# Up product of the gathered tokens: four expert blocks of a quarter's depth per weight slot in place of two of half the depth

## The chip, the cores and the metric

One core of one Trainium2 chip runs the kernel in one launch. The time is the device time of one execution in microseconds (us); several executions are timed and the median counts.

## What is computed

One step of a decoder layer with 2048 channels for 576 tokens: 512 of a prompt and 64 of eight samples. There are a pooling mixer and a retention mixer, a cross-attention to 256 memory tokens, and a PEER channel mixer. The change lies in the mixer of experts, which is cut here to what matters:

```python
q = (xb @ peer_wq).reshape(PEER_BLOCK, PEER_HEADS, 2, PEER_HALF)
s = jnp.einsum('thcd,hckd->thck', q, subkeys)
sv, si = lax.top_k(s, PEER_TOPK)
...
u = jnp.take(peer_u, expert, axis=0)
act = jax.nn.gelu(jnp.einsum('thkd,td->thk', u, xb), approximate=False)
vv = jnp.take(peer_v, expert, axis=0)
return jnp.einsum('thk,thkd->td', g * act, vv)
```

There are 8 heads and 16384 experts of one neuron each. The kernel doesn't gather rows of `peer_u`: it computes gelu(x u) for all experts, and picks what each token needs afterwards.

## The kernel before

**Tokens.** The first 320 tokens (ND) are dense: they go through all experts both up and down. The last 256 (NG) are "gathered": their up product is computed for all experts and stored in DRAM (`gelg`), from where single values are fetched by index, and their down product adds gathered rows of `peer_v` on VectorE. This text is about the up product of those 256 tokens. It takes place in the stage of the heads, on the tile `HLG`, which holds them as two column groups c of 128 tokens.

**Precision.** Every fp32 operand is split in a high part (fp32r) and a low part, and a product is three matmuls: high x high, high x low, low x high (the loop over wp and xp).

**The ring of weight slots.** All weights pass through four slots `WS[:, k]` of 128 partitions x 1024 columns, high and low. SyncE loads 512 KB into one of four raw buffers (two in `RAW`, one in `CS`, one in `AR`, `RAW3`) as soon as the slot four before has been split; ScalarE copies it to the high part (`high`, L902 to L908) once TensorE has released the slot (semaphore `used`) and the load has landed; GpSimd subtracts and writes the low part (`low_part`, L402 to L405); TensorE waits for `split_done`. ScalarE and GpSimd work in the order of the slots, and each instruction stands behind the one before it.

**The stage of the heads** (PE loop over EH = 8). For each head: two projections of queries, each over two slots, for all tokens (`projection`, moving tiles of 320 and 256 columns); the scores of the keys (L813, 20 small matmuls) in between; and an eighth of the expert blocks, 16 blocks of 128 experts, for the gathered tokens in `tokens_first` (L779 to L796). On VectorE the selection of the head's top 16 runs beside it (L1581 to L1628), after ScalarE has copied the scores (`sc_evac`).

In `tokens_first(h, j, hf)` a pair j of expert blocks takes four slots: SyncE loads for each block two slots, of channel halves 0 and 1 (`load_u` with `both_first`, so slots 0 and 1 hold half 0 of both blocks). TensorE moves 2 x 128 columns, the same 128 channels of both blocks out of two slots, past the stationary 128x128 tile of a token group:

```python
for wp, xp in ((0, 0), (0, 1), (1, 0)):
    ins = mm(to, HLG[:, c, xp, kb, :], WS[:, 2 * hf:2 * hf + 2, wp, k * P:(k + 1) * P], ...)
```

Both slots are needed at once and are released together. To refill them in time the handshake is by half slots: TensorE signals `used_q` after the first four of eight channel blocks, ScalarE copies the first 512 columns of both slots (`hi_q`), GpSimd splits these (`split_q`, L428), and then the second halves follow by `used`, `hi_done` and `split_done`. At the end of a pair ScalarE applies GELU to a bank of 512 columns (L1223) and stores 256 KB in `gelg` (L1225). There are 64 pairs, 8 per head (UPP).

**After it.** The softmax of the selected scores (ScalarE L1251, VectorE L1634 to L1636), nine transposes (L825), and then the stages of the dense tokens, in which GpSimd fetches values out of `gelg` (L440).

An older stage is used below for comparison, the projection of the memory values (L554): there the moving operand is 512 columns of a slot, 12 matmuls for each slot, and every slot is released alone.

## Time and profile before

| | |
|---|---|
| median of three runs | 4879.75 us (4876.03 to 4882.84) |
| profiled execution, its own time | 4868.53 us |
| span of its trace | 4866.4 us |
| mean granted clock of TensorE | 0.967 of full speed |
| TensorE matmuls, busy | 4551.1 us (94%), 31875 instructions |
| VectorE busy | 2297.8 us (47%) |
| ScalarE busy | 1584.6 us (33%) |
| GpSimd busy | 3099.6 us (64%) |
| matmuls of L793 | 6144, 740.5 us busy, 1788.7 to 2736.8 us (first and last start) |

Busy times are unions of an engine's instructions. A matmul's duration in the trace is its latency; matmuls overlap, so what one costs in a row of them is read from the distance of starts. In the timeline a row merges instructions of one line; the number in brackets is idle time ahead of it, with what ended it.

### The profile page before, as it was taken

The page shows a single profiled execution, that of the slowest core. Times are in us where ns is not written, and L with a number is a line of the kernel's source. Part 1 is how long each engine was busy: PE and PEld are TensorE (multiplying, and loading weights), DVE is VectorE, ACT ScalarE, POOL GpSimd, SP SyncE. Part 2 cuts the span into 40 slices and gives each one's busy share as a digit, 9 for nine tenths or more (in the row PEclk, how much of TensorE's full clock was granted, in tenths as well). Part 3 has the DMA queues.
Part 4 walks back from the last instruction along what each step waited for, and adds up shares of the span by engine and source line. Part 5 has one row for each costly group of instructions (what it writes and reads, how often), then busy time and mean ns, then how long its engine had stood idle before and what let it go on. Part 6 is the DMA issues. An engine that isn't in the chain of part 4 may idle for free.

```text
span 4866.4 us, 82443 instructions
## 1 busy us (share of the span) xinstructions
PE 4551.1 (94%) x31875; PEld 4401.3 (90%) x31875; DVE 2297.8 (47%) x3074; ACT 1584.6 (33%) x2194; POOL 3099.6 (64%) x1782
## 2 busy tenths in 40 slices
PE   7999999998998989999999888799999999999997
PEld 7799988897887979999999888799999999999997
DVE  3721322423001154444444555466666666666656
ACT  4422111222222134444444454233333333333333
POOL 6833222243221447777777766799999899998864
PEclk9999999999998999999999988899999999999998
DMA  6553222332555245555555556999999899999954
GB/s 217 191 93 103 97 97 87 107 120 105 186 200 177 83 146 173 173 173 172 173 174 174 156 158 176 334 342 344 344 342 346 322 347 341 341 344 357 347 187 140
DMA packets 466611, 1032.95 MB, mean 212 GB/s; under 512 B 136944, under 2 KB 227184, under 8 KB 433648
## 3 DMA queue, kind: packets, MB, share of 16 engines
q1 hardware_dynamic: 216080, 590.67, 36.1%
q0 software_dynamic: 45056, 268.60, 14.3%
q10 hardware_dynamic: 205280, 170.84, 10.8%
q8 instruction: 152, 2.49, 0.2%
q14 instruction: 43, 0.35, 0.0%
HBM read 935.25 MB, written 94.73 MB: 212 GB/s over the span
## 4 chain that ended last, share of the span: by engine, by line
issue 38%; POOL 35%; PE 18%; DMA 4%; DVE 2%; ACT 1%; another core or an unknown queue 1%; POOLq 0%; ACTq 0%; SPq 0%; DVEq 0%
POOL WS L404 23%; PE PS L864 9%; POOL WS L428 8%; PE PS L521 5%; POOL ROWS L450 3%; PE PS L793 2%; DMA AR<-in_vE 2%; POOL AR L440 2%; PE PS L839 2%; ACT WS L896 1%; DMA RAW<-in_vE 1%; DMA gel<-AR 0%; DVE AR L1371 0%; POOL AR L450 0%
## 5 line engine op out<-in xcount | busy, mean ns | idle before, releaser
L521 PE MATMUL PS<-HL,WS 128*128 128x288 f32 (+2 forms) x16896 | 2426.7, 304 | 127.3 <-DVE HL L1408 33.9
L521 PEld LDWEIGHTS PS<-HL,WS 128*128 128x128 f32 x16896 | 2371.5, 192 | 163.0 <-issue 110.4
L404 POOL TENSOR_TENSOR WS<-RAW,WS 128x1024 fp32r<-128x1024 f32 x490 | 1200.6, 2463 | 1354.7 <-ACT WS L896 1350.7
L864 PE MATMUL PS<-WW,WS 128*128 128x320 f32 x6144 | 941.8, 315 | 79.6 <-POOL WS L404 62.9
L864 PEld LDWEIGHTS PS<-WW,WS 128*128 128x128 f32 x6144 | 922.2, 192 | 98.6 <-issue 79.2
L896 ACT ACTIVATE WS<-RAW 128x1024 fp32r<-128x1024 f32 (+1 forms) x714 | 628.1, 919 | 1011.3 <-PE PS L521 360.2
L793 PE MATMUL PS<-WS,HL 128*128 128x256 f32 x6144 | 740.5, 283 | 0.0
L793 PEld LDWEIGHTS PS<-WS,HL 128*128 128x128 f32 x6144 | 738.3, 192 | 0.0
L1677 DVE SCALAR_TENSOR_TENSOR PS<-ROWS,AR,PS 128x2048 f32<-128x2048 f32 x206 | 483.8, 2349 | 77.1 <-DMA ROWS<-in_vE,AR 76.8
L404 POOL TENSOR_TENSOR WS<-AR,WS 128x1024 fp32r<-128x1024 f32 x182 | 452.3, 2489 | 42.6 <-ACT WS L896 41.7
L404 POOL TENSOR_TENSOR WS<-CS,WS 128x1024 fp32r<-128x1024 f32 x144 | 347.4, 2413 | 187.0 <-ACT WS L896 185.2
L1692 DVE TENSOR_TENSOR AR<-AR,PS 128x320 f32<-128x320 f32 x512 | 248.6, 486 | 435.7 <-PE PS L864 423.8
L896 ACT ACTIVATE WS<-CS 128x1024 fp32r<-128x1024 f32 (+1 forms) x256 | 223.0, 871 | 495.4 <-PE PS L864 257.2
L896 ACT ACTIVATE AR<-PS 128x512 f32<-128x512 f32 (+11 forms) x255 | 172.7, 719 | 560.5 <-PE PS L521 295.4
L428 POOL TENSOR_TENSOR WS<-RAW,WS 128x512 fp32r<-128x512 f32 x224 | 304.6, 1389 | 16.8 <-ACT WS L896 15.6
L896 ACT ACTIVATE WS<-AR 128x1024 fp32r<-128x1024 f32 (+1 forms) x294 | 259.8, 888 | 129.1 <-PE PS L521 53.3
L440 POOL DMA_INDIRECT AR<-gelg,AR x256 | 249.4, 974 | 70.6 <-issue 65.2
L1581 DVE MAX8 AR<-AR 128x8 f32<-128x128 f32 (+1 forms) x120 | 30.1, 324 | 488.8 <-ACT AR L896 487.6
L450 POOL DMA_INDIRECT ROWS<-in_vE,AR x206 | 200.2, 972 | 32.0 <-issue 25.5
L1232 ACT ACTIVATE AR<-PS 128x320 f32<-128x320 f32 x128 | 56.7, 443 | 449.9 <-PE PS L521 379.8
L1665 DVE TENSOR_TENSOR AR<-AR 128x320 f32<-128x320 f32 x128 | 193.9, 1566 | 0.1
L1677 DVE SCALAR_TENSOR_TENSOR PS<-AR,PS 128x2048 f32<-128x2048 f32 x50 | 117.6, 2353 | 115.4 <-DMA AR<-in_vE,AR 115.4
(160 smaller groups left out, 2883.3 us busy)
## 6 DMA issues: line engine op xcount, KB each, us to landing
RAW<-in_uT SPq DMA_DIRECT2D x256, 512.0 KB
RAW<-in_w_lin SPq DMA_DIRECT2D x218, 512.0 KB
CS<-in_uT SPq DMA_DIRECT2D x128, 512.0 KB
AR<-in_uT SPq DMA_DIRECT2D x128, 512.0 KB
RAW<-in_vE SPq DMA_DIRECT2D x128, 512.0 KB
CS<-in_vE SPq DMA_DIRECT2D x64, 512.0 KB
AR<-in_vE SPq DMA_DIRECT2D x64, 512.0 KB
AR<-in_w_lin SPq DMA_DIRECT2D x46, 512.0 KB
```

The source lines that it names most:

```text
L404: pool.tensor_tensor(WS[:, k, 1, :], raw(k, many, late), WS[:, k, 0, :].bitcast(F32), ALU.subtract)\
L428: pool.tensor_tensor(WS[:, k, 1, half], raw(k, True, True)[:, half], WS[:, k, 0, half].bitcast(F32), ALU.subtract).then_inc(S["split_done" ...
L440: pool.indirect_dma_start(out=GA[:, c, k:k + 1], out_offset=None, in_=values, in_offset=at(EL[:, c, k:k + 1]))\
L450: pool.indirect_dma_start(out=ROWS[b], out_offset=None, in_=rows, in_offset=at(VI[:, c, r:r + 1]))\
L521: ins = mm(to, WS[:, slot + hf, wp, k * P:(k + 1) * P], x, start=first and (wp, xp) == (0, 0), stop=last and wp == 1, skip_group_check=True)
L793: ins = mm(to, HLG[:, c, xp, kb, :], WS[:, 2 * hf:2 * hf + 2, wp, k * P:(k + 1) * P], start=(kb, c, wp, xp) == (0, 0, 0, 0), stop=kb == KB ...
L839: ins = mm(bank(4 + q % 2, P, off=P * k), BB[:, q % 2, k, :], AA[:, q % 2, k, :], start=True, stop=True, skip_group_check=True)
L864: ins = mm(bank(2 + d % 2, ND), WS[:, 2 * (q % 2) + b, vp, 512 * e + P * d4:512 * e + P * (d4 + 1)], W[:, 2 * b + e, wp, :], start=(b, e, ...
L896: copy = lambda out, in_, **kw: act.activation(out, in_, ACT.Identity, **kw)
L1665: tt(gi, gi, PP[:, e // 2, :, e % 2, :], ALU.mult).then_inc(S["w_done"], 1)
L1677: stt(ACC, ROWS[b], GA[:, c, r:r + 1], ACC, ALU.mult, ALU.add).then_inc(S["row_done"], 1)
L1692: tt(X[:, d, 0:ND], X[:, d, 0:ND], bank(2 + d % 2, ND), ALU.add).then_inc(S["v_free"], 1)
```

## The change

A quad j of four expert blocks now takes eight slots, and a slot holds a quarter of a half: 256 channels (two blocks of 128) of all four expert blocks. TensorE moves 4 x 128 = 512 columns out of one slot, past the same stationary tiles; each token group writes a bank of its own. There are 12 matmuls per slot, and the slot is released and refilled alone, through the same `used`, `hi_done` and `split_done` as elsewhere. The half-slot semaphores go. One GELU covers 1024 columns, and one store 512 KB. There are 32 quads, 4 per head (UPQ). The scores come after two slots, as before; ScalarE copies them after the high part that follows the third slot.

```diff
@@ SyncE
+            def load_quarters(quad, n):
+                for k in range(8):
+                    sp.wait_ge(S["split_done"], free(n + k, 4))
+                    sp.dma_start(raw(k % 4, True, True).rearrange("p (e w) -> p e w", e=4),
+                                 uT.rearrange("(b x) p w -> x b p w", x=2)[k // 4, bass.ds(4 * quad, 4), :, 256 * (k % 4):256 * (k % 4 + 1)]
+                                 .rearrange("b p w -> p b w")).then_inc(S[f"raw{k % 4}"], 16)
...
             with sp.Fori(0, EH - 1) as h:
-                load_u(h * (4 * UPP), h * H_HQ + (H_WQ + 4), 4 * UPP, both_first)
+                for j in range(UPQ):
+                    load_quarters(h * UPQ + j, h * H_HQ + (H_WQ + 4 + 8 * j))
@@ GpSimd
-            with pool.Fori(0, EH) as h:
-                for j in range(2):
-                    low_parts(h * H_HQ + (H_WQ + 4 * j), late=True)
-                for j in range(1, UPP):
...
-                                pool.tensor_tensor(WS[:, k, 1, half], raw(k, True, True)[:, half], WS[:, k, 0, half].bitcast(F32),
-                                                   ALU.subtract).then_inc(S["split_done" if at else "split_q"], 1)
+            with pool.Fori(0, EH * H_HQ // 4) as i:
+                low_parts(i * 4 + H_WQ, late=True)
@@ TensorE
-            def tokens_first(h, j, hf):
...
+            def tokens_first(h, j, quarters):
+                n = h * H_HQ + (H_WQ + 4 + 8 * j)
+                if quarters[0] == 0:
+                    pe.wait_ge(S["lin_evac"], h * (2 + UPQ) + (B_WQ + 2 + j + 1))
+                for q in quarters:
+                    pe.wait_ge(S["split_done"], n + split(q))
+                    for k in range(2):
+                        for c in range(2):
+                            for wp, xp in ((0, 0), (0, 1), (1, 0)):
+                                experts = WS[:, q % 4, wp, :].rearrange("p (e k n) -> p k e n", e=4, k=2)[:, k]
+                                ins = mm(tiles(bank(2 * (j % 2) + c)), HLG[:, c, xp, 2 * q + k, :], experts,
+                                         start=(q, k, wp, xp) == (0, 0, 0, 0), stop=(q, k, wp) == (7, 1, 1),
+                                         skip_group_check=True)
+                    ins.then_inc(S["used"], 1)
...
-                tokens_first(h, 0, 0)
+                tokens_first(h, 0, range(2))
...
-                tokens_first(h, 0, 1)
-                for j in range(1, UPP):
-                    for hf in range(2):
-                        tokens_first(h, j, hf)
+                tokens_first(h, 0, range(2, 8))
+                for j in range(1, UPQ):
+                    tokens_first(h, j, range(8))
...
-                    ins = pe.transpose(bank((3, 5, 6)[k], P, off=P * t), src[:, t, :], IDENT)
+                    ins = pe.transpose(bank(4 + k, P, off=P * t), src[:, t, :], IDENT)
@@ ScalarE
-                for hf in range(2):
-                    if j < UPP - 1:
-                        act.wait_ge(S["used_q"], h * (2 * UPP - 2) + (2 * j + hf + 1))
...
+                for q in range(8):
+                    act.wait_ge(S["used"], n + used(q + 1))
+                    high(n + (q + 4), q % 4, late=True)
+                    if (j, q) == (0, 2):
                         act.wait_ge(S["sk_done"], h + 2)
...
-                act.activation(GOG[:, e, :], bank(2 * e), ACT.Gelu).then_inc(S["lin_evac"], 1)
+                act.activation(GOG[:, e].rearrange("p s n -> p (s n)"), PS[:, 1024 * e:1024 * (e + 1)], ACT.Gelu)\
+                    .then_inc(S["lin_evac"], 1)
```

TensorE's order in the loop of the heads, from the last matmuls of the second query projection. L521 (L518 in the changed kernel) is the projection, L793 (L787) the up product, L813 (L805) the scores. Before:

```order
L521 MATMUL PS<-HL,WS 128x256
L783 REGISTER_ALU
L788 REGISTER_ALU
L793 MATMUL PS<-WS,HL 128x256 x48
L805 REGISTER_ALU
L806 REGISTER_ALU
L813 ISA
L813 MATMUL PS<-AR 128x128 x5
```

and in the changed kernel:

```order
L518 MATMUL PS<-HL,WS 128x256
L780 REGISTER_ALU
L782 REGISTER_ALU
L787 MATMUL PS<-WS,HL 128x512 x12
L782 REGISTER_ALU
L787 MATMUL PS<-WS,HL 128x512 x12
L797 REGISTER_ALU
L798 REGISTER_ALU
L805 ISA
L805 MATMUL PS<-AR 128x128 x5
```

48 matmuls of 256 columns over two slots have become twice 12 of 512 columns, with a wait ahead of each slot; the scores stand at the same slot. The rest of the head follows in the same manner, 12 matmuls per slot.

GpSimd's order in the same loop, with the waits: WS<-RAW, WS<-CS and WS<-AR are the subtractions for slots 0 and 1, 2, and 3. Before, from the second pair of a head on:

```order
L428 TENSOR_TENSOR WS<-RAW,WS 128x512 [waits hi_q]
L424 REGISTER_ALU
L428 TENSOR_TENSOR WS<-RAW,WS 128x512 [waits hi_q]
L426 REGISTER_ALU
L428 TENSOR_TENSOR WS<-RAW,WS 128x512 [waits hi_done]
L426 REGISTER_ALU
L428 TENSOR_TENSOR WS<-RAW,WS 128x512 [waits hi_done]
```

and in the changed kernel, the loop's whole body:

```order
L425 ISA
L413 TENSOR_TENSOR WS<-RAW,WS 128x1024 [waits hi_done]
L412 REGISTER_ALU
L413 TENSOR_TENSOR WS<-RAW,WS 128x1024 [waits hi_done]
L412 REGISTER_ALU
L413 TENSOR_TENSOR WS<-CS,WS 128x1024 [waits hi_done]
L412 REGISTER_ALU
L413 TENSOR_TENSOR WS<-AR,WS 128x1024 [waits hi_done]
L425 REGISTER_ALU
L425 COMPARE_AND_BRANCH
```

Four halves over two slots have become a whole slot each, and the loop turns every four slots, where it turned once per head.

## Rows read from the trace of the kernel before

**Rows 1.** stretches: us, busy us (count) of each engine, clock, DMA share, GB/s

```profile
1910.00:2030.00 120.00, 118.44 (x969) 118.26 (x968) 54.58 (x144) 49.88 (x81) 94.77 (x64) 1.00 0.55 176
150.00:226.00 76.00, 76.00 (x337) 62.93 (x336) 63.15 (x34) 38.73 (x47) 72.39 (x28) 1.00 0.64 210
```

**Rows 2.** groups, 1788 to 2740 us: shapes, count | busy us, mean ns | idle before

```profile
L793 PE MATMUL PS<-WS,HL 128*128 128x256 f32 x6144 | 740.5, 283 | 0.0
...
L428 POOL TENSOR_TENSOR WS<-RAW,WS 128x512 fp32r<-128x512 f32 x224 | 304.6, 1389 | 16.8 <-ACT WS L896 15.6
```

**Rows 3.** waits, 1788 to 2740 us: us in total, times, longest us

```profile
DVE AR L1581 <- ACT AR L896: 487.6, 8, 68.7
```

**Rows 4.** TensorE's timeline of one head: start us, us, operation, count [idle before]

```profile
2006.95 25.84 PE L521 MATMUL PS<-HL,WS 128*128 128x320 f32 x192 [1.56 <-issue]
2032.63 5.92 PE L793 MATMUL PS<-WS,HL 128*128 128x256 f32 x48
2038.38 2.39 PE L813 MATMUL PS<-AR 128*128 x20
2040.53 86.64 PE L793 MATMUL PS<-WS,HL 128*128 128x256 f32 x720
```

**Rows 5.** timeline of TensorE's weight loads in the value projection

```profile
149.87 76.12 PEld L554 LDWEIGHTS PS<-WS,HL 128*128 128x128 f32 x336
```

**Rows 6.** timeline of ScalarE and GpSimd, early in a head's expert slots

```profile
2033.53 1.07 ACT L896 ACTIVATE WS<-CS 128x1024 fp32r<-128x1024 f32 x1
...
2034.68 2.42 POOL L404 TENSOR_TENSOR WS<-CS,WS 128x1024 fp32r<-128x1024 f32 x1 [8.05 <-ACT WS L896]
...
2047.74 1.28 ACT L1223 ACT_TABLE_LOAD   x1
```

**Rows 7.** timeline of ScalarE and GpSimd in the value projection

```profile
163.43 1.01 ACT L896 ACTIVATE AR<-PS 128x1024 f32<-128x1024 f32 x1
163.82 5.26 POOL L404 TENSOR_TENSOR WS<-AR,WS 128x1024 fp32r<-128x1024 f32 x2
...
169.05 5.26 POOL L404 TENSOR_TENSOR WS<-RAW,WS 128x1024 fp32r<-128x1024 f32 x2
```

**Rows 8.** GpSimd's timeline during VectorE's one-hot work, first and last row

```profile
2076.08 3.79 POOL L428 TENSOR_TENSOR WS<-RAW,WS 128x512 fp32r<-128x512 f32 x2 [0.25 <-ACT WS L896]
...
2096.73 1.29 POOL L428 TENSOR_TENSOR WS<-AR,WS 128x512 fp32r<-128x512 f32 x1
```

**Rows 9.** timeline at the end of the stage

```profile
2737.19 1.06 ACT L896 ACTIVATE WS<-CS 128x1024 fp32r<-128x1024 f32 x1 [3.75 <-PE PS L793]
...
2739.10 0.58 ACT L1223 ACTIVATE AR<-PS 128x512 f32<-128x512 f32 x1
...
2742.45 0.82 DVE L1634 TENSOR_REDUCE AR<-AR 128x40 f32<-128x640 f32 x1 [32.60 <-ACT AR L1251]
...
2744.62 2.18 PE L825 MATMUL PS<-CST,AR 128*128 128x128 f32 x9 [7.55 <-DVE AR L1636]
...
2747.01 1.10 POOL L440 DMA_INDIRECT AR<-gelg,AR  x1 [4.03 <-DVE AR L1648]
```

**Rows 10.** DMA, 1788 to 2740 us: packets, MB, share; KB, us to landing

```profile
q1 hardware_dynamic: 40858, 148.82, 48.2%
q10 hardware_dynamic: 17136, 16.52, 5.3%
...
gelg<-AR ACTq DMA_DIRECT2D x64, 256.0 KB, 2.5
```

**Rows 11.** SyncE's timeline, two expert loads

```profile
1902.66 2.69 SPq L298 DMA_DIRECT2D RAW<-in_uT  x2
```

**Rows 12.** single microseconds (clock, DMA share, GB/s): key caches, expert loads

```profile
1388.00:1389.00 1.00, 1.00 1.10 350
...
1909.00:1910.00 1.00, 1.00 0.00 0
```

**Rows 13.** the page, GB/s in 40 slices of the span

```profile
GB/s 217 191 93 103 97 97 87 107 120 105 186 200 177 83 146 173 173 173 172 173 174 174 156 158 176 334 342 344 344 342 346 322 347 341 341 344 357 347 187 140
```

More of the change, by code:

```diff
@@ L66 @@
 QT = NQ - LAG // 2
-UPP = NP2 // EH
-H_HQ = 4 * (1 + UPP)
+UPQ = NQ // EH
+H_HQ = 4 + 8 * UPQ
 H_P = H_WQ + H_HQ * EH
@@ L72 @@
 H_ALL = H_V + 8 * (NQ - QT)
-B_P = B_WQ + (2 + UPP) * EH
+B_P = B_WQ + (2 + UPQ) * EH
 B_UV = B_P + 2 * NPG
@@ L272, in build @@
             "out_k0 out_k1 out_v0 out_v1 out_pool out_a out_spr out_sst out_b out_x out_om out_p0 out_p1 out_y out_g0 out_g1 "
-            "consts_set waited_v dve_step used hi_done split_done lin_evac used_q hi_q split_q "
+            "consts_set waited_v dve_step used hi_done split_done lin_evac "
             "sq_ready sq_used sum_done var_ready sd_ready t_ready hi_ready lo_ready "
@@ L363, in _, with load_u @@
             load_lin(H_MO + 4, H_WQ)
-            def load_u(half, n, count, order=(0, 1, 2, 3)):
+            def load_u(half, n, count):
                 for k in range(count):
-                    load(n + k, k % 4, uT[bass.ds(half + (k - k % 4 + order[k % 4]), 1)], late=True)
+                    load(n + k, k % 4, uT[bass.ds(half + k, 1)], late=True)
+            def load_quarters(quad, n):
[4 more added lines that the diff above has]
+                                 .rearrange("b p w -> p b w")).then_inc(S[f"raw{k % 4}"], 16)
             def load_v(i, n):
@@ L776, in _ @@
             norm_sum(3)
-            def tokens_first(h, j, hf):
-                n = h * H_HQ + (H_WQ + 4 + 4 * j)
-                if hf == 0:
-                    pe.wait_ge(S["lin_evac"], h * (2 + UPP) + (B_WQ + 2 + j + 1))
-                for k in range(KB // 2):
-                    if j and k == 0:
-                        pe.wait_ge(S["split_q"], h * (4 * UPP - 4) + (4 * j - 4 + 2 * hf + 2))
-                    if k == (4 if j else 0):
-                        pe.wait_ge(S["split_done"], n + split(2 * hf + 1))
-                    kb = hf * (KB // 2) + k
-                    for c in range(2):
-                        to = PS[:, 1024 * (j % 2) + NG * c:1024 * (j % 2) + NG * (c + 1)].rearrange("p (e n) -> p e n", e=2)
-                        for wp, xp in ((0, 0), (0, 1), (1, 0)):
-                            ins = mm(to, HLG[:, c, xp, kb, :], WS[:, 2 * hf:2 * hf + 2, wp, k * P:(k + 1) * P],
-                                     start=(kb, c, wp, xp) == (0, 0, 0, 0), stop=kb == KB - 1 and wp == 1,
-                                     skip_group_check=True)
-                    if k == 3 and j < UPP - 1:
-                        ins.then_inc(S["used_q"], 1)
-                ins.then_inc(S["used"], 2)
@@ L1202, in gelu_tokens @@
             def gelu_tokens(h, j):
[L1204 to L1217 removed]
+                n, e = h * H_HQ + (H_WQ + 4 + 8 * j), j % 2
+                for q in range(8):
+                    act.wait_ge(S["used"], n + used(q + 1))
+                    high(n + (q + 4), q % 4, late=True)
+                    if (j, q) == (0, 2):
                         act.wait_ge(S["sk_done"], h + 2)
@@ L1247, in _ @@
                     high2(h * H_HQ + (H_WQ + 2 * c + 4), 2 * c, late=True)
-                for j in range(UPP):
+                for j in range(UPQ):
                     gelu_tokens(h, j)
@@ L1254, in _ @@
             for k in range(3):
-                copy(GIJ[:, k, :], bank((3, 5, 6)[k], 3 * P))
+                copy(GIJ[:, k, :], bank(4 + k, 3 * P))
             copy(IOTA4, IOTA.unsqueeze(1).to_broadcast([P, 4, P])).then_inc(S["gt_evac"], 1)
@@ L1274, in _ @@
             for s in range(2):
[L1275 removed]
+                act.wait_ge(S[f"out_gg{s}"], 16 + 16 * (NQ // 2))
             def load_quad(i):
```

38 lines of the change are left out of this document (9 added, 29 removed).

## The prediction

> **What bounds the kernel now.** I read the table of stretches first, since the page's shares mix stages with different limits. In a stretch of 120 us inside the heads' stage (it lasts from 1788 to 2740 us) TensorE is busy 118.44 us at a granted clock of 1.00, the full 2.4 GHz of its two levels; GpSimd is busy 94.77, ScalarE 49.88, VectorE 54.58, and the DMA engines 0.55 of the time [rows 1]. So this stage lasts as long as its matmuls. The groups by line agree: L793 has no idle time ahead of it at all, while GpSimd waits for ScalarE [rows 2] and VectorE for ScalarE's score copy [rows 3]. TensorE's timeline of one head shows where 121.8 us go [rows 4]: 25.84 us of query projection, 5.92 us of up product, 2.39 us of scores (L813), then 720 matmuls of 256 columns in 86.64 us without a hole, and 1.56 us of "issue" at the loop's turn, the only idle time.
>
> **The matmuls.** What one costs is read from starts, since the duration of 283 ns is latency. 720 in 86.64 us, less 0.17 us by which the last one's end trails, is 120.1 ns each [rows 4]. 256 columns at 2.4 GHz are 106.7 ns, so 13.4 ns come on top. The price at 512 columns stands in another stage: the projection of the memory values (L554) sends 128x512 moving tiles from the same weight buffer past a 128x128 stationary tile, 12 matmuls per weight slot, as the new code does. From 149.87 us it issues 336 weight loads in 76.12 us at full clock; less the last load's 0.19 us that is 226.7 ns, where 213.3 would be the columns alone [rows 5]. Again 13.4 ns on top. The alternating 320 and 256 columns of the query projection agree: 192 in 25.84 us, 133.7 ns after the same correction for the tail, against 120.0 of columns. So the extra goes by the instruction. The change makes 3072 matmuls of 512 columns out of 6144 of 256: 6144 x 120.1 = 737.9 us become 3072 x 226.7 = 696.4 us, **41.5 us less**, if nothing makes TensorE wait.
>
> The Trainium skill speaks against this size ("TensorE: Matmul & The Clock Gate", section "Wait — 56ns, not 53.3ns?"): beside the columns, a back-to-back matmul is said to cost only about 2.5 ns. By that rule halving the count would give 3072 x 2.5 = 7.7 us. The rows above show 13.4 ns at both widths and I go by them; the rule's case is a rival below.
>
> **The ring of weight slots.** 288 slots of 512 KB pass through this stage before and after: 32 of queries and 256 of expert weights. Before, a pair of blocks took two slots at once, so one expert slot was 737.9 / 256 = 2.88 us of TensorE; now it is 12 x 226.7 = 2.72 us, and each is released alone. Following one slot: TensorE's release reaches ScalarE in some 0.2 us, its copy of 1024 columns takes 1.07, GpSimd's subtraction 2.42, the two starting 1.15 apart [rows 6], so a slot is ready 3.8 us after its release. TensorE wants it three slots later, after 3 x 2.72 = 8.2 us: **4.4 us of cover**. That is also why I cost the removal of the half-slot handshakes (used_q, hi_q, split_q) at nothing: they hid a refill of two slots together behind the other two, which the new order does not need. If that cover is gone, GpSimd's pace is what is paid (rival B).
>
> **GpSimd.** Two subtractions of 512 columns (1389 ns each in the mean [rows 2]) become one of 1024, 2.42 us where VectorE is quiet [rows 6]. Of 2.72 us that is 89%. Its loop now turns every four slots instead of every 36; the value projection has such a loop too, and there GpSimd's pairs follow each other every 5.2 us across the turns, 2.6 us per slot, with no idle time [rows 7], VectorE busy 63.15 of 76 us beside it, and TensorE busy all 76 [rows 1]. So I put zero for the turns. The dense spot is VectorE's one-hot work: from 2076.08 to 2097.99 us GpSimd made 14 halves, 3.13 us per slot [rows 8], slower than the new 2.72 and also than the old 2.88. Over 7 slots it falls 7 x 0.41 = 2.9 us behind, less than the 4.4 of cover, and then catches up. Zero, but with the least room of all terms.
>
> **ScalarE.** Two half highs become one of 1.07 us [rows 6]. One GELU of 1024 columns replaces two of 512 (0.58 each [rows 9]); by the copy of 128x1024 out of PSUM in the value projection it takes 1.01 us [rows 7], so high and GELU are 2.1 us, within a slot. At a head's first GELU a table load of 1.28 us is added [rows 6]: 0.6 us late, covered. The score copy comes after the third slot instead of the first two, so VectorE's work of a head starts some 2.3 us later; VectorE sat idle 487.6 us in 8 waits there, 61 per head [rows 3]. In the last head it had 32.6 us to spare [rows 9]; the token part gets 5.2 us shorter and it starts 2.3 later, so 25 remain. At the stage's end ScalarE had two highs left (1.06 us each) and a GELU of 0.58 ahead of the softmax's exponential, for whose result TensorE waited 7.55 us [rows 9]. Now it is one high and a GELU of 1.01: 2.07 instead of 2.70, **0.6 us less**, on the path. The store of gelg is 512 KB instead of 256 and lands perhaps 1.5 us later; the gathers that need it start at 2747.0, 7 us after the last GELU's end [rows 9], and such a store lands within 2.5 us of its issue [rows 10]. Zero.
>
> **DMA.** SyncE's queue keeps 256 loads of 512 KB in place and order, each issue now cut into runs of 1 KB (four blocks by 256 columns) instead of 4 KB. The rate asked is 512 KB in 2.72 us, 193 GB/s, against 182 before. Nothing queues behind them on SyncE but the next load, which waits for the same split. The key caches are loaded in 1 KB packets: 350 GB/s in a full microsecond [rows 12]. And 16.52 MB of stores by the second queue (17136 packets, about 1 KB) cost 5.3% of 16 engines' time, as much per byte as the 148.82 MB of long packets for 48.2% [rows 10]. A raw slot is free at the split, 3.8 us after TensorE's release, and wanted 10.9 after it: 7.1 us. Two loads issued from 1902.66 us on, the second at the end of a row of 2.69 us [rows 11], had nothing left to move from 1909 on [rows 12], so one needs about 4. What no row shows is the address pattern, 1 KB out of every 4 KB and four blocks 1 MB apart; value blocks are read as 2 KB out of 8, in a stage that moves 342 to 357 GB/s in most of its slices [rows 13]. I take no cost, between 0 and half the rate (rival D).
>
> **After the stage** nothing changes but three bank numbers; everything moves forward together. The bounds of the sum: no more than 41.5 + 0.6 can come from this. **Sum: 42.1 us less.** The profiled execution took 4868.5 us (span 4866.4), so its like would take 4826.4; the median of the runs is 11.2 us above it, and the forecast is given against that: 4879.75 - 42.1 = **4837.6 us**.
>
> **The rivals.**
> **B. GpSimd in VectorE's one-hot stretch becomes the bound.** If cover is used up (a table load, a late slot) when the stretch begins, all 2.9 us per head are paid: 8 x 2.9 = 23 us, 4861. For it: 3.13 against 2.72 us, 89% load otherwise. Against: 4.4 us of cover, and before, at 3.13 against 2.88, no wait of L793 appears. Chance 0.15, mostly as a part of it.
> **C. The extra goes by columns or mostly so.** If the operand cut in four runs, or the wider result, costs as much per column as today, 512 columns cost 240.2 ns and the stage gains nothing: 4879. Against: 226.7 [rows 5]. For: that tile was contiguous. Chance 0.04. By the 2.5 ns of the Trainium skill's page named above it would be 4872, on the same side of the bound.
> **D. Slower: the strided loads.** If 1 KB runs at a 4 KB pitch reach half of 350 GB/s, 175, a slot takes 524288 / 175000 = 3.00 us and the DMA sets the pace: 256 x 3.00 = 768 us, 30 more than now, 4910. It decides from 182 GB/s down; between 193 and 182 it only eats the gain. For it: no row has this pattern. Against: the two rates above [rows 12, 13]. The Trainium skill ("DMA: Bandwidth & Descriptors", section "Latency and other measured facts") reports copies slowed by row pitches that are large powers of two, at 2 MiB by a fifth and at 4 MiB by half, not at 512 KiB; no run here shows that, and the 1 MB step between blocks lies between those. Chance 0.05.
>
> **How the numbers follow.** Forecast 0.76, B 0.15, C 0.04, D 0.05. Faster by over 0.2% (9.8 us, about what a measurement can tell here) are the forecast and B, 0.91; C is within it, 0.04; D is slower, 0.05. The range: the three runs before spread over 7 us, and 42 us less with that spread gives 4831 to 4844; the high end goes to 4858 to hold nearly all of B; C and D are left out with 0.09. The low end is 4829, since no term can give more.
>
> **What would show it.** In the changed profile: 3072 matmuls of 128x512 with about 697 us busy and no idle time; one head 121.8 - 5.2 = 116.6 us; GpSimd's pieces 2.4 us, up to 3 in the one-hot stretch; DMA share still near 0.55. B would show as idle of the new line released by GpSimd's split, some 45 to 70 us after each head's first expert slot; D as ScalarE's highs waiting for DMA in nearly every slot; C as a spacing near 240 ns. The forecast is wrong if the stage's first to last matmul is not close to 948 - 42 = 906 us.

## The result, and the profile after

The median went from 4877.89 us (4875.43 to 4882.84, 4 runs) to **4819.83 us** (4813.65 to 4822.48, 4 runs), a ratio of 0.9878 with an interval of 0.9861 to 0.9895, which is 51 to 68 us less (58.1 by the medians). The forecast was 42.1 us less. The profiled execution took 4813.65 us (span 4811.5); against the profiled one of before that is a span 54.9 us shorter.

The table of stretches of the changed kernel, a head's stage and the value projection, in the columns of [rows 1]:

```profile
1900.00:2015.00 115.00, 115.00 (x599) 99.98 (x598) 62.79 (x144) 46.87 (x49) 89.78 (x36) 1.00 0.59 182
...
150.00:226.00 76.00, 76.00 (x337) 62.94 (x336) 63.75 (x34) 38.65 (x47) 72.04 (x28) 1.00 0.63 209
```

The untouched value projection is as before. In the stage of the heads TensorE is now busy all 115 us; before it was 118.44 of 120. VectorE is busier, 63 of 115 us against 55 of 120, and nothing in the change gives it more work. The groups of the stage (1786 to 2690 us), in the columns of [rows 2]:

```profile
L787 PE MATMUL PS<-WS,HL 128*128 128x512 f32 x3072 | 700.1, 389 | 0.0
L787 PEld LDWEIGHTS PS<-WS,HL 128*128 128x128 f32 x3072 | 575.5, 188 | 118.9
L413 POOL TENSOR_TENSOR WS<-RAW,WS 128x1024 fp32r<-128x1024 f32 x142 | 347.6, 2458 | 103.3 <-ACT WS L887 102.5
L1605 DVE TENSOR_TENSOR AR<-AR 128x256 f32<-128x256 f32 x80 | 203.3, 2610 | 0.3
```

L787 stands where L793 stood: 740.5 us busy [rows 2] became 700.1, 40.4 less, and no idle time ahead of it. That is not all of the 54.9. TensorE's timeline over a head's turn, to be held against [rows 4]:

```profile
2016.38 5.63 PE L787 MATMUL PS<-WS,HL 128*128 128x512 f32 x24
2021.84 2.39 PE L805 MATMUL PS<-AR 128*128 x20
2023.99 81.88 PE L787 MATMUL PS<-WS,HL 128*128 128x512 f32 x360
2105.71 25.76 PE L518 MATMUL PS<-HL,WS 128*128 128x320 f32 x192
2131.30 5.63 PE L787 MATMUL PS<-WS,HL 128*128 128x512 f32 x24
```

360 matmuls in 81.88 us, less 0.16 us for the last one's tail (389 - 227 ns), are 227.0 ns each; 226.7 were forecast. But the row of the projection (L518) no longer has a bracket: the 1.56 us of "issue" at the loop's turn are gone. A head takes 114.9 us (2016.38 to 2131.30), not the 116.6 forecast; before, it took 121.9 (2006.95 to 2128.87).

Where the 54.9 us of span went, by first and last instructions of each part in the two traces: first to last matmul of the up product 948.0 us (1788.8 to 2736.8) to 893.6 (1786.5 to 2680.1), **54.4 less**; start of the stage 2.3 earlier; last up product to first transpose (L825, now L816) 7.8 to 7.4; all that follows 2.2 longer (2121.7 to 2124.0). The start of the stage is scatter: in the runs below, which leave what precedes it alone, it begins between 1779.4 and 1796.0. So the gain is in the stage, and its 54.4 us are 40.4 of matmuls and **14.0 of something that the prediction did not have**.

The seven turns of the loop of heads had holes of 1.84, 1.56, 1.70, 2.13, 1.96, 1.54 and 1.51 us before, 12.2 together. The view doesn't count as idle the 0.16 us by which the latency of the last matmul (283 ns) outlasts its 120, so in starts they are 13.4. Each projection after a hole is also 0.08 us longer (25.84 us against 25.76), 0.6 in all, and that closes the sum: 14.0. What differs with them is a DMA queue that neither the rows nor the text of the prediction looked at. Queue q8 carries the engines' instructions. Over the up product's stretch the kernel before had

```profile
q8 instruction: 69, 1.13, 0.4%
```

and the changed kernel, in the view of the same name (queue, kind: packets, MB, share of 16 engines):

```profile
q1 hardware_dynamic: 136758, 148.42, 54.0%
q8 instruction: 3, 0.05, 0.0%
```

66 packets of 16.4 KB are gone. Three of them are gone because TensorE's whole program is shorter by three packets (see "Where it begins" below); the other 63 are nine for each of the seven turns, and the trace of before shows nine between any two turns (9 from 2006.95 to 2128.87 us, and 9 in each of its neighbours). TensorE's loop body of a head, counted from the built programs with a matmul and its weight load as two, was 1995 instructions and is 1225. It begins at the same place of TensorE's program in both. So besides being wider, the matmuls became fewer in a loop that the engine had been fetching anew at each turn. That is a theory at this point: the handshakes, the order of slots and the number of waits changed too.

The end of the stage, in the timeline of all engines, to be held against [rows 9]:

```profile
2680.62 1.06 ACT L887 ACTIVATE WS<-AR 128x1024 fp32r<-128x1024 f32 x1 [1.66 <-PE PS L787]
2681.59 1.01 ACT L1205 ACTIVATE AR<-PS 128x1024 f32<-128x1024 f32 x1
...
2685.36 0.82 DVE L1617 TENSOR_REDUCE AR<-AR 128x40 f32<-128x640 f32 x1 [14.12 <-ACT AR L1234]
...
2687.54 2.18 PE L816 MATMUL PS<-CST,AR 128*128 128x128 f32 x9 [7.03 <-DVE AR L1619]
...
2689.92 1.10 POOL L437 DMA_INDIRECT AR<-gelg,AR  x1 [5.82 <-DVE AR L1631]
```

One high and one GELU stand ahead of the exponential, and TensorE waits 7.03 us instead of 7.55, 0.5 less where 0.6 were forecast. VectorE's room in the last head is 14.1 us and not the 25 forecast (32.6 before).

### The profile page after: what moved, and what is told of

Read it like the earlier page. It is cut to its first block, busy times and chain, and to the rows that moved or that the text cites. A ratio compares the mean times of both kernels' runs of the same rounds, so it can differ in the third digit from the quotient of the medians.

```text
span 4811.5 us, 75763 instructions
## 1 busy us (share of the span) xinstructions
PE 4511.4 (94%) x28803; PEld 4239.8 (88%) x28803; DVE 2369.8 (49%) x3074; ACT 1558.3 (32%) x1938; POOL 3055.9 (64%) x1558
## 4 chain that ended last, share of the span: by engine, by line
PE 37%; issue 28%; POOL 25%; DMA 4%; DVE 3%; another core or an unknown queue 2%; ACT 1%; ACTq 0%; POOLq 0%; DVEq 0%; SPq 0%
POOL WS L413 20%; PE PS L787 14%; PE PS L518 12%; PE PS L855 9%; POOL ROWS L447 3%; DMA AR<-in_vE 2%; POOL AR L437 2%; PE PS L830 1%; ACT WS L887 1%; DMA RAW<-in_vE 1%; DVE AR L1380 1%; DVE AR L1354 1%; DMA gel<-AR 0%; POOL AR L447 0%
## 5 line engine op out<-in xcount | busy, mean ns | idle before, releaser
L518 PE MATMUL PS<-HL,WS 128*128 128x288 f32 (+2 forms) x16896 | 2426.6, 304 | 118.9 <-DVE HL L1391 33.9
L518 PEld LDWEIGHTS PS<-HL,WS 128*128 128x128 f32 x16896 | 2370.0, 191 | 154.0 <-issue 102.8
L413 POOL TENSOR_TENSOR WS<-RAW,WS 128x1024 fp32r<-128x1024 f32 x602 | 1476.2, 2463 | 1353.3 <-ACT WS L887 1347.7
L887 ACT ACTIVATE WS<-RAW 128x1024 fp32r<-128x1024 f32 x602 | 617.6, 1055 | 999.9 <-PE PS L518 359.1
L787 PE MATMUL PS<-WS,HL 128*128 128x512 f32 x3072 | 700.1, 389 | 0.0
L787 PEld LDWEIGHTS PS<-WS,HL 128*128 128x128 f32 x3072 | 575.5, 188 | 118.9
L413 POOL TENSOR_TENSOR WS<-AR,WS 128x1024 fp32r<-128x1024 f32 x238 | 599.7, 2523 | 52.0 <-ACT WS L887 51.1
L413 POOL TENSOR_TENSOR WS<-CS,WS 128x1024 fp32r<-128x1024 f32 x200 | 492.2, 2461 | 195.4 <-ACT WS L887 193.5
L887 ACT ACTIVATE WS<-CS 128x1024 fp32r<-128x1024 f32 x200 | 211.6, 1058 | 417.7 <-PE PS L855 265.8
L887 ACT ACTIVATE WS<-AR 128x1024 fp32r<-128x1024 f32 x238 | 249.9, 1055 | 202.7 <-PE PS L787 92.8
L1605 DVE TENSOR_TENSOR AR<-AR 128x256 f32<-128x256 f32 x80 | 203.3, 2610 | 0.3
```

The source lines that it names most:

```text
L413: pool.tensor_tensor(WS[:, k, 1, :], raw(k, many, late), WS[:, k, 0, :].bitcast(F32), ALU.subtract)\
L518: ins = mm(to, WS[:, slot + hf, wp, k * P:(k + 1) * P], x, start=first and (wp, xp) == (0, 0), stop=last and wp == 1, skip_group_check=True)
L787: ins = mm(tiles(bank(2 * (j % 2) + c)), HLG[:, c, xp, 2 * q + k, :], experts, start=(q, k, wp, xp) == (0, 0, 0, 0), stop=(q, k, wp) == (7 ...
L887: copy = lambda out, in_, **kw: act.activation(out, in_, ACT.Identity, **kw)
L1605: ins = tt(v, v, SIF[:, c, t, :].unsqueeze(1).to_broadcast([P, TOPK, TOPK]), ALU.mult)
```

## The experiments

Theories: **body**, the 14 us are the fetching of a loop body that is too long, and go with its number of instructions; **form**, they come from the new order and handshakes; **width**, the matmuls' 40 us come from 512 columns for each. Each run was timed beside runs of the kernel before on its own chip, which had medians of 4808.11 us in the first group (e1 to e4), 4811.24 in the second (e5 to e8) and 4810.27 in the third (e9 to e11), so ratios are compared, not times. Four runs (e6 to e8, and in part e4) ask after other steps of the prediction: GpSimd's cover and the strided loads.

### The kernel before with a shorter body

```diff
@@ TensorE, kernel before
-                for j in range(1, UPP):
-                    for hf in range(2):
-                        tokens_first(h, j, hf)
+                with pe.Fori(0, UPP // 2 - 1) as i:
+                    for j in (1, 2):
+                        for hf in range(2):
+                            tokens_first(h, j, hf, i)
+                for hf in range(2):
+                    tokens_first(h, UPP - 1, hf)
```

> The kernel before, with matmuls of 256 columns and the half-slot handshake, where TensorE's six middle pairs of a head are an inner loop of three turns over two pairs. The body of the heads falls from 1995 to 1212 instructions; the work is the same. Theory F: no holes at the turns, 4877.9 - 12 = 4866 us, and few instruction packets in the stage. Rival G: the holes stay, 4878 us. If a turn of an inner loop costs TensorE something itself, 24 more turns would show as holes in the middle of a head.

Measured: 4793.09 us, ratio 0.9969 (0.9957 to 0.9982). First to last up product 934.2 us, 13.8 less than in the trace of before, with the same 740.5 us of 6144 matmuls. Its timeline and its instruction queue:

```profile
1999.61 25.76 PE L521 MATMUL PS<-HL,WS 128*128 128x320 f32 x192
2025.21 5.92 PE L793 MATMUL PS<-WS,HL 128*128 128x256 f32 x48
2030.98 2.39 PE L813 MATMUL PS<-AR 128*128 x20
2033.12 86.64 PE L793 MATMUL PS<-WS,HL 128*128 128x256 f32 x720
```

```profile
q8 instruction: 3, 0.05, 0.0%
```

The up product and the scores take what they take in [rows 4] to a hundredth, the projection takes 25.76 us instead of 25.84, and the hole is gone. The handshakes, the order and the widths are those of before; the inner loop turns three times per head without a gap that shows. So the 14 us belong to the body, not to the form: 13.8 here against the 14.0 looked for.

### The changed kernel with matmuls of 256 columns

```diff
@@ TensorE, changed kernel
-                                ins = mm(tiles(bank(2 * (j % 2) + c)), HLG[:, c, xp, 2 * q + k, :], experts, ...)
+                                for half in range(2):
+                                    ins = mm(tiles(bank(2 * (j % 2) + c))[:, 2 * half:2 * half + 2], HLG[:, c, xp, 2 * q + k, :],
+                                             experts[:, 2 * half:2 * half + 2], ...)
```

> The changed kernel where each matmul of 512 columns is two of 256 over the same weights slot and bank, each with its own weight load. Slots, loads, GELU, ScalarE and GpSimd are those of the changed kernel; the body has 1993 instructions. Against the first kernel of this job (same body size, 512 columns) only the width differs. Theory of the prediction (13.4 ns per instruction beside the columns): 3072 x 13.4 = 41 us more than that kernel, so 4873 us, spacing 120.1 ns. Rival C (the extra goes by columns): the same time as that kernel, 4832 us.

Measured: 4809.90 us, ratio **0.9998** (0.9989 to 1.0007): all of the gain is gone. 952.7 us from first to last, 740.5 busy, 69 packets in q8, and the seven holes are back with 13.8 us:

```profile
2005.69 25.84 PE L518 MATMUL PS<-HL,WS 128*128 128x320 f32 x192 [2.18 <-ACT AR L1207]
2031.37 5.92 PE L788 MATMUL PS<-WS,HL 128*128 128x256 f32 x48
2037.13 2.39 PE L807 MATMUL PS<-AR 128*128 x20
2039.27 86.64 PE L788 MATMUL PS<-WS,HL 128*128 128x256 f32 x720
2127.93 27.36 PE L518 MATMUL PS<-HL,WS 128*128 128x320 f32 x192 [2.02 <-issue]
```

The new loads, one-slot handshakes, GELU of 1024 columns and order of GpSimd are all in it and are worth nothing together. In the list of seven the bracket names "issue" three times, ScalarE's GELU three times and GpSimd once, for holes of one kind. The projection does not wait for that GELU: in the changed kernel it starts at 1990.78 us, before the GELU of the same turn (1992.03), and in the hole that is put down to GpSimd it starts at 2495.89, while the GELU runs (2495.43 to 2496.44). The last row shows that such a hole can cost more than its length. The projection after it takes 27.36 us instead of 25.84, and the stretches say why (us, TensorE's busy us and count, clock, DMA share, GB/s):

```profile
2129.00:2131.00 2.00, 2.00 (x10) 0.50 0.98 324
2131.00:2133.00 2.00, 2.00 (x16) 0.89 0.89 270
```

After the 2.02 us without a matmul the granted clock was at its lower level, 1.2 GHz, for a while. The same happened after the hole of 1.89 us at the last turn; after the other five, and after all seven of the kernel before (up to 2.13 us), the projection took its 25.8 us; the longest of them, 2.18 us, was one of these. Take from this run's 952.7 us its holes (13.8, and 7 x 0.24 in starts, as above) and the 3.0 of the two slow projections, and 934.2 are left, as in the previous run, which has the old handshakes. So the form makes no difference. **The width is worth 40.6 us** (934.2 - 893.6, both without holes), the forecast 41.5. The comparison that was planned, with the run of 768 added waits, fell through: that run was slowed by its waits and is the longer one (982.3 us, next section).

### The changed kernel with the body padded

Waits that are always satisfied, on semaphores that have long passed the value, between the up product's matmuls. Several names fold into one instruction; what counts is the number of instructions added.

```diff
@@ TensorE, changed kernel, in the loop over wp and xp of tokens_first
+                                for name in ("consts_set", "in_const"):
+                                    pe.wait_ge(S[name], 2)
```

(This adds one instruction per matmul, 384 in a head. With five names it adds two per matmul, 768; the runs between have five at some matmuls and two at the rest. In the last run there are two or three added instructions at each of the first 288 matmuls of a head and none at the last 96.)

> The changed kernel with 768 instructions added to TensorE's loop over the heads that do no work: waits on semaphores that were reached long before. The loop's body then has 1993 instructions (a matmul and its weight load counted as two), as the kernel before had 1995; the changed kernel has 1225. Everything else is the changed kernel. Theory F (code fetch: a body of 1995 is fetched anew at each turn of the loop, one of 1225 stays): the seven holes of 1.5 to 2.1 us at the turns come back, 12.2 us in all, with some 60 packets of instructions in the stage, so 4819.8 + 12 = 4832 us. Rival G (the holes belonged to the handshake by half slots or to the loads of the old form): no hole, 4820 us. Rival H (the time beyond the forecast is scatter between executions): the holes may be there or not, and the time stays within 4 us of the changed kernel's.

> The same with 384 added instructions, a body of 1609. It controls the price of the added waits themselves and brackets the size at which the fetch begins. Theory F: the retention loop of 1781 is fetched anew at its turns by the count of instruction packets, the loop of 975 is not; at 1609 I expect no hole and 4820 us, with few packets (under 10) in the stage; if the fetch begins below 1609, holes as in the other kernel and 4832. Rival G: no hole. If the added waits cost time themselves, the matmuls' spacing rises above 227 ns in both kernels.

> The changed kernel with 608 added instructions of TensorE in the body, 1833 in all, spread so that a matmul has two of them ahead of it six times in ten and one otherwise. In the kernel with 768 of them the matmuls themselves came slower (243.6 ns apart against 227), so that its time did not show the holes alone; with 384 they did not (227). Theory F: at 1833 instructions the code is fetched anew (the retention loop of 1781 is), the seven holes come back with about 60 packets, and the spacing stays at 227 ns; first to last matmul of the up product 893.6 + 12 to 14 = 906 to 908 us, ratio to the kernel before 0.988 + 0.0027 = 0.991. If the fetch begins only above 1833: no holes, 893.6 us, 0.988.

> The changed kernel with 511 added instructions that only wait (always satisfied) in TensorE's loop of heads: a body of 1736. In TensorE's program it starts at instruction 8499. Packets of the instruction queue were 16.4 KB each in the runs so far; at 64 bytes an instruction, 256 in a packet, that body lies in 7 blocks (33 to 39, to 8499 + 1736 = 10235 of 10240), as the one of 1609 did. Theory blocks (a body is fetched anew when it touches 8 blocks or more, kept when it touches 7): no holes at the turns, about 5 packets of the instruction queue in the stage, 893.6 us from first to last up product, ratio about 0.988. Rival length (it goes by the number of instructions, with a limit somewhere between 1609 and 1781 that can as well be 1700): it may be fetched anew, 69 packets, seven holes of 0.3 to 0.7 us, 896 to 898 us.

> The same with 535 added instructions, a body of 1760, 24 more than in the run before: it ends at 10259 and touches block 40, so 8 blocks. Theory blocks: 69 packets of the instruction queue and seven holes of 0.3 to 1.0 us, some 897 us from first to last up product, ratio about 0.990, though it has only 1.4 per cent more instructions than the run with 1736. Rival length: the same answer as the run with 1736 unless the limit lies by chance between the two.

> The changed kernel with a body of 1993 instructions, like the run with 768 added waits (holes of 3.7 to 4.1 us) and the kernel before (1.5 to 2.1 us), but here all 768 stand in the first three of a head's four quads, two or three per matmul, and the last 96 matmuls before the loop's turn have none. Theory run-ahead (TensorE's sequencer issues ahead of the array where there are few instructions per us, and the refetch at the turn is hidden by what was issued ahead; in the run with 768 evenly spread, at 61 ns an instruction, nothing was ahead): 69 packets again, but holes of at most 0.6 us, and likely less than the 0.4 to 1.0 of the body of 1833. Rival size (the hole grows with the body's length): 1.5 to 4 us, as the other two bodies of 1993 to 1995. In both the first three quads are slower than 227 ns a matmul, at 4 to 5 instructions of 61 ns: 270 to 300 ns, so up to 8 x 288 x 0.06 = 138 us more in the stage, ratio 1.01 to 1.03; the time of this run tells nothing, its holes do.

| run | body | ratio (interval) | first to last, us | matmuls busy, us | holes, us (each) | q8 packets |
|---|---|---|---|---|---|---|
| the change | 1225 | 0.9878 (0.9861 to 0.9895) | 893.6 | 700.1 | none | 3 |
| e2 | 1609 | 0.9884 (0.9869 to 0.9899) | 893.6 | 700.1 | none | 5 |
| e9 | 1736 | 0.9877 (0.9856 to 0.9898) | 893.5 | 700.1 | none | 5 |
| e10 | 1760 | 0.9879 (0.9860 to 0.9898) | 893.6 | 700.1 | none | 6 |
| e5 | 1833 | 0.9902 (0.9888 to 0.9916) | 899.6 | 700.0 | 4.4 (0.42 to 1.01) | 69 |
| e1 | 1993 | 1.0071 (1.0057 to 1.0085) | 982.3 | 748.4 | 26.9 (3.68 to 4.06) | 69 |
| e11 | 1993 | 1.0279 (1.0252 to 1.0306) | 1090.6 | 886.6 | 3.8 at six turns (0.39 to 1.01), none at the seventh | 69 |

**Where it begins.** 535 added waits cost nothing, so waits as such don't. Between 1760 and 1833 instructions the body begins to be fetched anew, and it is the same 69 packets as in the kernel before, nine between turns. The guess that it goes by blocks of 256 in the program fell: the bodies of 1736 and 1760 end on either side of such a boundary, as counted, and neither was fetched. The retention loop of the same program, whose body has 1781 instructions, probably belongs to it too. At 256 instructions a packet TensorE's program of 16,268 instructions fills 64, which leaves 22 of the profile's 86 packets over; for the kernel before it is 17,038 and 67, and 67 + 22 + 63 are its 152. The retention loop has two turns, with "issue" of 0.78 and 0.90 us. That the 22 are its own is inferred and not shown. If they are, and if a loop's place in the program doesn't matter, the onset lies between 1760 and 1781.

**What a turn costs.** Two bodies of 1993 have holes of 26.9 us and of 3.8 us in all. With 768 waits spread evenly, TensorE's timeline shows

```profile
2019.40 27.35 PE L518 MATMUL PS<-HL,WS 128*128 128x320 f32 x192 [3.86 <-POOL WS L413]
```

and with the same number kept out of the last 96 matmuls (21.8 us) before the turn

```profile
2032.74 25.83 PE L518 MATMUL PS<-HL,WS 128*128 128x320 f32 x192 [0.43 <-issue]
```

So the hole does not go by the body's length, and the rival that said so is out. What differs is how fast TensorE had to take its instructions just ahead of the turn. In the run with 3.86 us the matmuls are 243.6 ns apart (748.4 / 3072), with four instructions for each, 61 ns an instruction: the instructions set the pace, and nothing can be ahead of the array when the fetch begins. In the run with 0.43 us two instructions go into 227 ns. This fits instructions that are taken ahead and cover most of the fetch. So do the first 24 matmuls after each projection in the run with 3.86 us: 5.63 us, 227 ns each, though they too have waits between them. No run shows the taking ahead by itself, so this part is argued. The kernel before lies between with 1.5 to 2.1 us, and its two instructions per 120.1 ns are close to 61 ns each. What it does not explain is the remainder: at six of seven turns 0.4 to 1.0 us stayed in that run, as in the one with 1833, and less was expected.

The run with 768 even waits was meant as a clean test of the body and is none, since the matmuls became slower too; it shows that the fetching comes back and not what it costs by itself. That is 6.0 us at 1833 instructions (899.6 - 893.6), half of the 12 to 14 expected, and 13.8 in the form of before. In the last run the first three quads, with 4.7 instructions per matmul, are slow; the ratio is in the range expected (1.01 to 1.03), but they are slower than 61 ns an instruction gives: 308 ns a matmul against 270 to 300, and 197 us more in the stage against at most 138. Only its holes are read.

### Contiguous loads

```diff
@@ SyncE, changed kernel, load_quarters
-                    sp.dma_start(raw(k % 4, True, True).rearrange("p (e w) -> p e w", e=4),
-                                 uT.rearrange(...)[k // 4, bass.ds(4 * quad, 4), :, 256 * (k % 4):256 * (k % 4 + 1)] ...)
+                    sp.dma_start(raw(k % 4, True, True), uT[bass.ds(8 * quad + k, 1)].rearrange("a p n -> p (a n)"))
```

> The changed kernel whose 256 loads of expert weights read 4 KB runs (whole rows of the stored blocks) in place of 1 KB runs at a 4 KB pitch. The slots then hold other experts' columns than the products assume, so the values of the up product for the gathered tokens are not those of the reference; the amount of data and all instructions are. Theory: loads were hidden, so the time is the same, 0.988 of before, first to last 893.6 us; the DMA share in the stage falls from 0.59 to 0.55 and the packets of the first queue from 136758 to about 40600. Rival D in a weak form (strided loads cost something somewhere): up to 5 us less.

Measured: 4750.89 us, ratio 0.9874 (0.9859 to 0.9889), 893.6 us from first to last. Its queue, from 1788 to 2680 us:

```profile
q1 hardware_dynamic: 40773, 148.48, 56.2%
```

40773 packets instead of 136753 and about the same share (56.2% against 54.1%) of the DMA engines, rather more than less. So runs of 1 KB at a pitch of 4 KB out of four blocks 1 MB apart cost nothing at this rate: rival D is out by more than its effect on the time. The expectation that the share falls back to 0.55 was wrong. 0.59 over 115 us is not the price of short runs; with contiguous loads the same stretch has 0.60, at 182 GB/s in both. What raises the share is open.

### GpSimd held up, and GpSimd in halves

Three subtractions of 1024 columns to unused places, once per head, ahead of the low part of slot 29 (slots counted from the head's first):

```diff
@@ GpSimd, changed kernel
+                    if j == 7:
+                        pool.wait_ge(S["hi_done"], h * H_HQ + (H_WQ + 4 * j + 1))
+                        for n in range(3):
+                            pool.tensor_tensor(..., raw(0, True, True), raw(0, True, True), ALU.subtract)
```

> The changed kernel with three more subtractions of 1024 columns on GpSimd, 7.2 us, once per head ahead of the 29th of its 36 slots (they write to memory that is free then). It measures the cover of the slot ring, which the forecast put at 4.4 us. If the cover is 4.4: TensorE waits 7.2 - 4.4 = 2.8 us in each head, 22 us in all, first to last 893.6 + 22 = 916 us, ratio 0.992. If it is all hidden the cover is over 7.2 us: 0.988. If there is no cover at that place: 58 us, 1.000.

Measured: 4791.08 us, ratio 0.9953 (0.9938 to 0.9968), 927.7 us from first to last, 34.1 more. The timeline of one head's delay:

```profile
1967.25 2.58 POOL L413 TENSOR_TENSOR WS<-AR,WS 128x1024 fp32r<-128x1024 f32 x1
...
1967.89 1.06 ACT L893 ACTIVATE WS<-RAW 128x1024 fp32r<-128x1024 f32 x1 [1.66 <-PE PS L793]
1969.79 4.12 POOL L430 TENSOR_TENSOR AR<-RAW 128x1024 f32<-128x1024 f32 x2
...
1973.87 2.07 POOL L430 TENSOR_TENSOR WW<-RAW 128x1024 fp32r<-128x1024 f32 x1
1975.90 5.05 POOL L413 TENSOR_TENSOR WS<-RAW,WS 128x1024 fp32r<-128x1024 f32 x2
...
1978.48 11.89 PE L793 MATMUL PS<-WS,HL 128*128 128x512 f32 x44 [2.55 <-POOL WS L413]
...
1983.23 1.06 ACT L893 ACTIVATE WS<-RAW 128x1024 fp32r<-128x1024 f32 x1 [5.21 <-DMA RAW<-in_uT]
```

6.1 us of extra work (1969.79 to 1975.90) became a hole of 2.55 us, the same in all eight heads (20.5 us in the groups). So **3.6 us of cover** lay there, where the prediction had 4.4. The first two rows account for the rest: the high part was ready at 1968.95 and GpSimd, beside VectorE's work, got to it at 1969.79, 0.84 us late by its own backlog. This is what rival B would have looked like: a bracket that names GpSimd, in every head, at the same slot, and ScalarE waiting for its load later, since the raw slot had come free late. No run without the added work shows it. The other 13.6 us of the 34.1 are in the matmuls' busy time, 713.7 against 700.1, and the clock accounts for them (the columns of [rows 1]):

```profile
1975.00:1978.00 3.00, 0.93 (x5) 0.43 (x3) 3.00 (x2) 1.95 (x2) 3.00 (x2) 1.00 0.00 0
1978.00:1981.00 3.00, 2.52 (x8) 2.02 (x9) 3.00 (x2) 0.02 (x1) 3.00 (x3) 0.79 0.62 172
1981.00:1984.00 3.00, 3.00 (x10) 2.38 (x9) 2.86 (x3) 0.77 (x1) 3.00 (x2) 0.64 1.03 334
1984.00:1990.00 6.00, 6.00 (x29) 4.94 (x28) 0.25 (x1) 2.41 (x3) 6.00 (x3) 1.00 0.69 210
```

After a pause of 2.55 us TensorE had part of the next 5.5 us at the lower clock, 1.7 us per head on top (13.6 / 8).

The other run gives GpSimd its old pieces back, two of 512 columns per slot:

```diff
@@ GpSimd, changed kernel
+                    for half in (slice(0, HW // 2), slice(HW // 2, HW)):
+                        ins = pool.tensor_tensor(WS[:, k, 1, half], raw(k, True, True)[:, half],
+                                                 WS[:, k, 0, half].bitcast(F32), ALU.subtract)
+                    ins.then_inc(S["split_done"], 1)
```

> The changed kernel where GpSimd makes each low part of the stage in two instructions of 512 columns, as the kernel before did, with one signal at the end. In the changed kernel VectorE's one-hot multiplications took 2610 ns each instead of 1505, while GpSimd's instructions became 2.4 us long instead of 1.3. Theory P (VectorE's instruction waits for the end of GpSimd's running one): with halves the multiplications fall back to about 1500 ns and VectorE's idle time per head grows from 47 to about 61 us, and the total stays, 0.988 of before, since neither engine bounds the stage; GpSimd needs 2.5 instead of 2.4 us per slot. Rival: the 2610 ns come from the higher DMA share; then they stay.

Measured: 4753.44 us, ratio 0.9875 (0.9860 to 0.9890), 893.6 us, as the changed kernel. Its groups:

```profile
L429 POOL TENSOR_TENSOR WS<-RAW,WS 128x512 fp32r<-128x512 f32 x280 | 360.1, 1317 | 86.5 <-ACT WS L892 86.5
...
L1610 DVE TENSOR_TENSOR AR<-AR 128x256 f32<-128x256 f32 x80 | 114.5, 1501 | 0.3
```

VectorE's one-hot multiplications of 256 columns take 1501 ns beside pieces of 512 and 2610 beside pieces of 1024. Their own width did not change (L1605 in the second fence of this text). The rival was the DMA share, and it is out: it is 0.58 here and 0.59 in the changed kernel. So the length of GpSimd's instructions draws these VectorE instructions out, and the lost room in the last head comes from it, since with halves the room is back:

```profile
2690.52 0.82 DVE L1622 TENSOR_REDUCE AR<-AR 128x40 f32<-128x640 f32 x1 [27.08 <-ACT AR L1239]
```

It is not a rule for every instruction: 40 other multiplications of the same shape (L1606, now L1589) went the other way, from 1460 ns to 415, and take 632 with halves.

The time of the kernel does not hang on it: TensorE never waits for VectorE in the heads but at the end, and there is room there.

No run beats the changed kernel: with contiguous loads, with halves or with bodies up to 1760 the intervals lie on that of the change.

## Why the prediction was right and wrong

**The direction, and most of the size.** The forecast's one large term held: 41.5 us from 3072 matmuls at 226.7 ns. Measured are 40.4 by the busy times, 40.6 by the two forms without holes, and a spacing of 227.0. What the matmul costs at 512 columns was read from another stage of the same trace [rows 5], and this was right to 0.3 ns, although there the operand lies in one piece and here in four. Rival C is out. By the 2.5 ns of the Trainium skill ("TensorE: Matmul & The Clock Gate", section "Wait — 56ns, not 53.3ns?") 7.7 us would have come of it; the runs give five times that.

**What failed: the hole at the turn.** The step is the sentence on [rows 4], where 1.56 us of "issue" are "the only idle time". The text saw them, gave them no cause, left them in the new head ("121.8 - 5.2 = 116.6 us") and then said "no more than 41.5 + 0.6 can come from this". That bound was taken over the terms that the change was meant to touch. The hole was the refetching of a body of 1995 instructions, and a change that halves the number of matmuls takes 770 instructions out of that body. Missing were 13.8 us (the run with the shorter body alone), which with 41.5 and 0.6 makes 55.9 against 54.9 of span. The low end of the range, 4829, rested on the same sentence and had no room for it. The data lay in the profile: the diff had 6144 matmuls become 3072 in a loop of eight, and the third part of the page has a queue named "instruction" with 152 packets over the span, where the changed kernel has 86.

The Trainium skill has the mechanism ("Runtime: NRT & Kernel Launch", section "Instruction fetch mechanics"): TensorE's instruction memory holds 2048 instructions, is refilled in blocks of 256, and a taken branch to what lies outside a window of two blocks must fetch before going on. The trace agrees on the blocks (16.4 KB a packet) and on the stall at a turn. It does not agree on the size at which this begins: 1833 instructions were fetched anew in this loop, 1760 were not. By that page's 2048 the body of 1995 would have fitted, and by its two blocks not even the one of 1225 would.

**The cover of 4.4 us** was right for a GpSimd without backlog; where it was measured, 3.6 were left. It was enough, so the zeros stand, that for the 7 x 0.41 us of the dense stretch too, and rival B did not occur.

**VectorE's room** in the last head: 25 us forecast, 14.1 there. The term had counted when it starts, and not that longer GpSimd pieces draw out its instructions. It cost nothing, but was the zero with the least behind it.

**The loads**: no cost, right; the share of 0.55 to stay, wrong by 0.04 and without consequence. The store of gelg lands in 5.5 us at the median against 2.5, so 3.0 later and not 1.5; the gathers wait for VectorE (5.82 us above), not for it. **ScalarE's end of the stage**: 0.6 forecast, 0.5 measured. The 2.2 us that the stages behind lost have no term in the sum and may be scatter: in two runs of one group, of 1736 and of 1760 instructions, the same stages took 2066.8 and 2059.4 us.

## What to carry to other kernels

Before a bound is set on what a change can give, every idle row on the path needs a cause, a hole of "issue" at a loop's turn above all: count the instructions of the loop body for its engine before and after, and look at the packets of the instruction queue over the loop's stretch. A body near the engine's limit can be cut for nothing by an inner loop (0.9969 for the kernel before, by a few lines). And the price of a wider instruction is best taken from another stage of the same trace in which that width is already used.

## What was not expected of the hardware

- A loop body of TensorE of 1760 instructions was kept, one of 1833 was fetched anew at every turn, in nine packets of 16.4 KB a turn. The turn then cost up to 4.1 us, by what goes ahead of it and not by the body's length. Why 0.4 to 1.0 us stay at most turns in the best case, and nothing at one of seven, is open.
- Waits that are satisfied cost nothing at up to 3.6 instructions per 227 ns (the body of 1833, in the mean); four instructions for each matmul took 243.6 ns, some 61 ns an instruction, and 4.7 took 308, some 66. At 256 columns two instructions take 120.1 ns, nearly that rate. So whether the 13.4 ns beyond the columns there are the matmul's own or this rate can't be said; at 512 columns, two instructions in 227 ns, it can't be the rate.
- VectorE's one-hot instruction of 128x256 took 1501 ns beside GpSimd pieces of 512 columns and 2610 beside pieces of 1024; another of the same shape took 632 and 415.
- After pauses of 2.55 us TensorE's granted clock fell to its lower level for a while in every head (1.7 us lost). After pauses of 1.5 to 2.2 us it did so in two cases of fourteen, at 2.02 and 1.89 us, though one of 2.18 did not bring it.
